# Compression weights of the second mixer: read unsplit as fp32 moving operands, with the block rows in four 32-column groups of the array

## The reference, cut to what matters

```python
def nsa_compress(k, pos, w1, w2):
    n_cmp = (seq - CMP_LEN) // CMP_STRIDE + 1            # 15
    idx = np.arange(n_cmp)[:, None] * CMP_STRIDE + np.arange(CMP_LEN)[None, :]
    blk = jnp.swapaxes(k[:, idx], 2, 3) + pos.astype(k.dtype)
    flat = blk.reshape(bsz, n_cmp, g, CMP_LEN * dk)      # 2 groups x 15 windows = 30 rows of 2048
    return jax.nn.gelu(flat @ w1, approximate=True) @ w2  # w1: 2048 x 256
```

## Time and profile before

| what | value |
| --- | --- |
| time, median of 3 runs | 2051.24 us (2049.7 to 2053.11) |
| span of the profiled execution | 2053.3 us, 2.1 us over that median |
| TensorE busy | 2039.6 us, 99% of the span |
| VectorE, ScalarE busy | 1475.2 us (72%), 1152.8 us (56%) |
| granted TensorE clock, mean | 0.998 |

### The profile page before, as it was taken

The page is one execution under the profiler, slowest core; times in us unless marked ns, Lnnn a source line. Parts: engine busy times, 40 slices in busy tenths (PEclk is TensorE's granted clock), DMA queues, the critical chain, the costliest instruction groups (busy, mean ns, idle before and its releaser), DMA issues.

```text
span 2053.3 us, 39877 instructions
## 1 busy us (share of the span) xinstructions
PE 2039.6 (99%) x17337; PEld 1975.7 (96%) x17340; DVE 1475.2 (72%) x1877; ACT 1152.8 (56%) x1459; POOL 129.9 (6%) x114
## 2 busy tenths in 40 slices
PE   9999999999999999999999999999999999999998
PEld 8999899999999999999999999999999999999998
DVE  6556866655655587676557999678778899868776
ACT  5435365534544456564446776756557685756555
POOL 1001000100101010010000000001000000000100
PEclk9999999999999999999999999999999999999999
DMA  7665544666566565366665554455655564445652
GB/s 256 206 206 175 183 144 141 196 198 195 175 207 200 190 193 165 103 200 221 223 200 168 163 165 140 159 175 186 223 191 156 162 199 160 149 151 171 222 186 103
DMA packets 287106, 369.78 MB, mean 180 GB/s; under 512 B 10531, under 2 KB 258771, under 8 KB 286931
## 3 DMA queue, kind: packets, MB, share of 16 engines
q1 hardware_dynamic: 281858, 361.47, 54.1%
q10 hardware_dynamic: 5072, 5.75, 0.9%
HBM read 365.36 MB, written 1.05 MB: 178 GB/s over the span
## 4 chain that ended last, share of the span: by engine, by line
PE 96%; DVE 1%; ACT 1%; DMA 1%; ACTq 0%; issue 0%; DVEq 0%
PE ps L717 28%; PE ps L718 27%; PE ps L719 27%; PE ps L828 1%; PE ps L889 1%; PE ps L887 1%; PE ps L885 1%; PE ps L1259 1%; PE ps L830 1%; PE ps L829 1%; DMA arena<-arena 1%; PE ps L1271 1%; PE ps L1292 1%; ACT whi L1482 1%; PE ps L1079 1%; PE ps L1106 0%
## 5 line engine op out<-in xcount | busy, mean ns | idle before, releaser
L717 PE MATMUL ps<-hhi,whi 128*128 128x256 f32 x3774 | 1056.2, 280 | 1.4 <-DVE hlo L2221 1.3
L718 PE MATMUL ps<-hlo,whi 128*128 128x256 f32 x3774 | 1044.1, 277 | 0.0
L719 PE MATMUL ps<-hhi,wlo 128*128 128x256 f32 x3774 | 1044.0, 277 | 0.0
L2128 DVE TENSOR_TENSOR wlo<-raw,whi 128x2048 fp32r<-128x2048 f32 x341 | 771.9, 2264 | 376.6 <-ACT whi L1482 376.5
L1482 ACT ACTIVATE whi<-raw 128x2048 fp32r<-128x2048 f32 (+2 forms) x346 | 651.4, 1886 | 537.1 <-PE ps L719 441.9
L717 PEld LDWEIGHTS ps<-hhi,whi 128*128 128x128 f32 x3774 | 707.6, 187 | 9.0 <-issue 5.4
L718 PEld LDWEIGHTS ps<-hlo,whi 128*128 128x128 f32 x3774 | 707.7, 188 | 1.2 <-issue 0.5
L719 PEld LDWEIGHTS ps<-hhi,wlo 128*128 128x128 f32 x3774 | 708.0, 188 | 0.2
L717 PE MATMUL ps<-hidhi,whi 128*128 128x256 f32 x880 | 243.3, 276 | 0.0
L719 PE MATMUL ps<-hidhi,wlo 128*128 128x256 f32 x880 | 243.1, 276 | 0.0
L718 PE MATMUL ps<-hidlo,whi 128*128 128x256 f32 x880 | 243.1, 276 | 0.0
(11 more groups left out here) (321 smaller groups left out, 2189.6 us busy)
## 6 DMA issues: line engine op xcount, KB each, us to landing
raw<-in_ffn_w_up SPq DMA_DIRECT2D x88, 1024.0 KB, 5.2
raw<-in_w_in SPq DMA_DIRECT2D x68, 1024.0 KB, 5.2
raw<-in_ffn_w_down SPq DMA_DIRECT2D x66, 1024.0 KB, 5.0
raw<-in_ffn_w_gate SPq DMA_DIRECT2D x43, 1024.0 KB, 5.3
raw<-in_w_gate SPq DMA_DIRECT2D x32, 1024.0 KB, 5.4
raw<-in_w_branch SPq DMA_DIRECT2D x16, 1024.0 KB, 5.0
raw<-in_nsa_cmp_w SPq DMA_DIRECT2D x8, 1024.0 KB, 5.4
raw<-in_w_out SPq DMA_DIRECT2D x6, 1024.0 KB, 5.0
```

Of the source, the lines that this page charges most:

```text
L717: pe.matmul(o, w_hi, m_hi, start=start, stop=False, skip_group_check=True)
L718: pe.matmul(o, w_hi, m_lo, start=False, stop=False, skip_group_check=True)
L719: return pe.matmul(o, w_lo, m_hi, start=False, stop=stop, skip_group_check=True)
L2128: dve.tensor_tensor(wlo[:, slot, 0:n], raw[:, slot, 0:n], whi[:, slot, 0:n].bitcast(F32), ALU.subtract) \
```

## The change

For units 15 to 18 the split is gone: TensorE reads the weights from `raw`, in plain fp32, as the moving operand, and the block rows from `blkf` unsplit, in plain fp32, as the stationary one. One matmul takes the place of three. The eight slices of a unit go in turn to four groups of 32 output partitions of the PSUM bank, so each of four groups of columns of the array holds the rows of its own slices. The four partial sums then stand below one another (126 partitions): ACT copies them out, and the matmul that turned the 30 rows now also adds the four groups, since its moving operand is four identity matrices stacked (`quads`, a new constant). The gelu moves behind the turn.

SP's loads into the slots that these units held wait for `used` (TensorE is done) and no longer for `lo_ready`. The semaphore counts for the later splits are shifted (`splits2`). `pool_avg` moves to another part of its buffer, so that it does not lie over `blkf`.

```diff
+PLAIN_UNITS = tuple(range(M2_W1, M2_GATE))
+QUAD = 32
...
+    quads = (r[:, None] % QUAD) == np.arange(QUAD)[None, :]
...
-        pool_avg = view(pool_flat[:, 3072:4096], g=4, t=SEQ)
+        pool_avg = view(pool_flat[:, 0:1024], g=4, t=SEQ)
...
+            def load2(l, s, n, src):
+
+                slot = s % RING
+                if s - RING in PLAIN_UNITS:
+                    sp.wait_ge(used[slot], uses2(l, s))
+                    sp.dma_start(raw[:, slot, 0:n].rearrange("p (k c) -> p k c", k=src.shape[1]), src) \
+                        .then_inc(raw_ready[slot], 16)
+                else:
+                    load(slot, n, splits2(l, s), src)
...
                     if i == M2_W1:
-                        pe.wait_ge(blk_split, (l + 1) * 2)
-                    slot = i % RING
-                    unit_ready(slot, u(i))
-                    o = bank(4, v * CMP_HID, CMP_HID)[0:KVH * NCMP, :]
+                        pe.wait_ge(blk_ready, (l + 1) * BLK_STEPS)
+                    slot, rows = i % RING, KVH * NCMP
+                    pe.wait_ge(raw_ready[slot], 16 * (uses2(l, i) + 1))
                     for jl in range(CJ // 2):
-                        j = part * (CJ // 2) + jl
-                        w = slice(jl * CMP_HID, (jl + 1) * CMP_HID)
-                        b = slice(j * KVH * NCMP, (j + 1) * KVH * NCMP)
-                        last = mm3(o, blk_hi[:, v, b], blk_lo[:, v, b], whi[:, slot, w], wlo[:, slot, w], j == 0, j == CJ - 1)
+                        j, q = part * (CJ // 2) + jl, jl % 4
+                        n = QUAD if q < 3 else rows
+                        b = (v * CJ + j) * rows
+                        last = pe.matmul(bank(4, v * CMP_HID, CMP_HID)[q * QUAD:q * QUAD + n, :], blk_flat[:, b:b + n],
+                                         raw[:, slot, jl * CMP_HID:(jl + 1) * CMP_HID], start=j < 4, stop=j >= CJ - 4,
+                                         skip_group_check=True)
                     last.then_inc(used[slot], 1)
...
-                    pe.wait_ge(gelu_done, l * 3 + 1)
+                    pe.wait_ge(hid_kept, l + 1)
                     n = KVH * NCMP
                     for x in range(4):
-                        last = pe.matmul(bank(4, x * 32, n), hid_tok[0:n, x * P:(x + 1) * P], ident[0:n, 0:n], start=True, stop=True)
+                        last = pe.matmul(bank(4, x * QUAD, n), hid_tok[0:HID_ROWS, x * P:(x + 1) * P], quads[0:HID_ROWS, 0:n],
+                                         start=True, stop=True)
...
                 def next_split(i):
+                    if i + 2 in PLAIN_UNITS:
+                        return
...
-                        act.activation(hid_tok[0:KVH * NCMP, :], bank(4)[0:KVH * NCMP, :], ACT.Gelu_apprx_tanh).then_inc(gelu_done, 1)
+                        act.activation(hid_tok[0:HID_ROWS, :], bank(4)[0:HID_ROWS, :], ACT.Copy).then_inc(hid_kept, 1)
...
-                    if i == BLK_AT:
-                        for v in range(2):
-                            act.wait_ge(blk_ready, l * BLK_STEPS + (v + 1) * BLK_STEPS // 2)
-                            act.activation(blk_hi[:, v, :], blkf[:, v, :, :, :].rearrange("p j g n -> p (j g n)"), ACT.Copy) \
-                                .then_inc(blk_hi_done, 1)
...
-                                       .rearrange("p x (g n) -> p x g n", g=KVH), ACT.Copy).then_inc(gelu_done, 1)
-                        act.wait_ge(gelu_done, l * 3 + 2)
+                                       .rearrange("p x (g n) -> p x g n", g=KVH), ACT.Gelu_apprx_tanh).then_inc(gelu_done, 1)
+                        act.wait_ge(gelu_done, l * 2 + 1)
```

More of the change, by code:

```diff
@@ L88 @@
 POOL_AT = 15
-BLK_AT = 9
 CONV_FROM = 7
@@ L164 @@
                       ("causal", 3 * P), ("window", 3 * P), ("cmpadd", TT * CP), ("cmp01", TT * CP),
-                      ("blockdiag", P), ("half", 2)])
+                      ("blockdiag", P), ("half", 2), ("quads", QUAD)])
 POOL_COLS = SEQ + P
@@ L387, in hybrid_network @@
         on_half = table(C2_AT, "half", 2)
+        quads = table(C2_AT, "quads", QUAD)
         def par_rows(i, r, n, src):
@@ L526, in uses2, with splits2, unsplit @@
             return DEPTH * (L1_UNITS // RING) + l * (L2_UNITS // RING) + s // RING
+        def splits2(l, s):
+            def unsplit(before):
+                return sum(x % RING == s % RING for x in PLAIN_UNITS if x < before)
+            return uses2(l, s) - l * unsplit(L2_UNITS) - unsplit(s)
         def bank1_of(i):
@@ L626, in conv_load @@
                 def conv_load(s, src):
-                    load(s % RING, UNIT, uses2(l, M2_END + s), src)
+                    load2(l, M2_END + s, UNIT, src)
                 def gate(p):
@@ L686, in _ @@
                         src = A["nsa_cmp_w1_2"][bass.ds(l, 1), v, part * D:(part + 1) * D, :]
-                        load(s % RING, UNIT, uses2(l, s), src.rearrange("a (j p) c -> p (a j) c", p=P))
+                        load2(l, s, UNIT, src.rearrange("a (j p) c -> p (a j) c", p=P))
                         s += 1
@@ L695, in _ @@
                                 .rearrange("k p c -> p k c")
-                        load(s % RING, UNIT, uses2(l, s), src)
+                        load2(l, s, UNIT, src)
                         s += 1
@@ L700, in _ @@
                         src = w[bass.ds(l * (NBR * BRC * P) + (n * BRC * P + i * UC), UC), :]
-                        load(s % RING, UNIT, uses2(l, s), src.rearrange("(k p) c -> p k c", p=P))
+                        load2(l, s, UNIT, src.rearrange("(k p) c -> p k c", p=P))
                         s += 1
-                out_proj(l, uses2, s, A["w_o_2"])
+                out_proj(l, splits2, s, A["w_o_2"])
                 conv_ffn(l)
@@ L2728, in turn @@
                                                       ALU.add).then_inc(blk_ready, 1)
-                def blk_low():
-                    for v in range(2):
-                        dve.wait_ge(blk_hi_done, l * 2 + v + 1)
-                        dve.tensor_tensor(blk_lo[:, v, :], blkf[:, v, :, :, :].rearrange("p j g n -> p (j g n)"),
-                                          blk_hi[:, v, :].bitcast(F32), ALU.subtract).then_inc(blk_split, 1)
                 def softmax(j):
```

45 lines of the change are left out of this document (23 added, 22 removed).

## The result

The changed kernel takes 2055.11 us (median of 9 runs, 2051.55 to 2057.86), beside 2051.18 us of the kernel before (9 runs). The ratio is 1.0017 with a 95% interval of 1.0009 to 1.0025: **slower by 3.9 us**, 1.8 to 5.1. It is inside the forecast's range, 4.7 us above its point, and on the slower side of no change, by a small amount that the interval does tell from zero.

A forecast was written before the change was run, and what follows sets the result against it. TensorE, busy 99% of the span, bounds the kernel. Of 13.3 us saved in matmuls, late loads leave 0.4 us a layer, 0.8 us for two: 2050.4 us, own range 2048.5 to 2054.0, over the cases 2046.0 to 2056.5.

The forecast's parts named there:

- What the matmuls give: Units 15 to 18 on TensorE: four groups at once, 1.1 us a unit, 1.66 us saved, 13.3 us over eight.
- rival (c): Units 15 to 18: one column group at a time, 3.7 us a unit, +13.8 us, 2065.0 us; chance 0.06.
- What the moved loads cost: Unit 19's load 1.0 us later, 4 us wait at `times_v(0)`, unit 20 0.8 us early, 0.4 us a layer kept.
- that half: Half of unit 20's 0.8 us lead taken as kept, 0.4 us a layer, since VectorE is 98% busy until 1240.
- The removed splits: Eight high parts on ScalarE, eight low parts on VectorE and the block rows' split: by themselves worth nothing.
- The clock: Behind the `times_v(0)` wait the clock may fall to half: one fall +0.6 us, two +2.1 us; verdict unmoved.
- both fall: The clock falls behind the `times_v(0)` wait in both layers: +2.1 us, 2053.3 us.
- (a): The gain arrives because the waits do not come; all of it gives 2037.9 us; chance 0.13.
- (b): Units 15 to 18: only two groups at once, 2.0 us a unit, +3.7 us, 2054.9 us; chance 0.12.
- (d): The clock falls in both layers at its full price, 3.4 us each, 2056.4 us; chance 0.06.
- The base: The profiled span of 2053.3 us stood 2.1 us over the runs' median; the forecast step was taken from 2051.24.

The follow-up runs named there:

- Experiment 4: The changed kernel with all eight matmuls of a unit in one column group instead of four; 2068.23 us, ratio 1.0087.
- experiment 1: The changed kernel with filler matmuls, 16 ahead of `times_v(0)` and 2 ahead of `hidden_turn`; 2051.24 us, ratio 0.9999.
- experiment 7: The changed kernel with the 16 filler matmuls ahead of `times_v(0)` alone, none at `hidden_turn`; 2049.61 us, ratio 0.9993.
- experiment 8: The changed kernel with unit 19's weights loaded into the free buffer `mixed`, ahead of unit 18's load; 2043.81 us, ratio 0.9962.
- experiment 2: The changed kernel with ScalarE's split of unit 19 moved behind the tanh that `times_v(0)` waits for; 2052.32 us, ratio 1.0005.
- experiment 5: The changed kernel with unit 16's weights in the free buffer `mixed`, unit 19's load issued right behind unit 18's; 2053.35 us, ratio 1.0007.
- experiment 6: The changed kernel with the early loads of experiment 5 and the ScalarE order of experiment 2 together; 2051.15 us, ratio 0.9996.
- experiment 9: The kernel of experiment 8 with ScalarE's split of unit 19 also moved behind its tanh; 2048.78 us, ratio 0.9988.
- experiment 10: The kernel before, weights split and three passes kept, with only the early load of unit 19 from experiment 8; 2051.59 us, ratio 1.0001.
- experiment 3: The changed kernel with `pool_windows` put behind unit 16 instead of ahead of it; 2050.32 us, ratio 0.9993.

## Why the prediction was wrong, step by step

**What the matmuls give: right.** 1.1 us a unit predicted, 1.00 measured. Four groups at once was an assumption beyond the rows, which showed two; it came true. Experiment 4 gives the price without the groups, 3.6 us a unit, and 6.8 to 7.0 us a layer where rival (c) had 6.9.

**What the moved loads cost: right, to 0.1 us in layer 0, as long as the clock holds.** Counted from unit 15, the load of unit 19 goes out at 5.80 us (predicted 5.9), its split starts at 11.23 (11.3), `times_v(0)` at 15.18 (15.1), behind a wait of 4.07 (4). From there on the kernel with fillers shows the same program with the clock holding: unit 19 at 18.60 us (predicted 18.6, from 1186.35), unit 20 at 27.46 (27.46, from 1195.2; 27.80 in layer 1), and VectorE's low part of unit 22 at 34.53 (34.46, from 1202.2). The lead at unit 22 is 0.5 and 0.4 us, where I had taken 0.4 a layer; that half was a choice between 0 and 0.8, so its fit is partly luck. Experiments 1 and 7 are 0.9 and 1.1 us below the kernel before, where I had 0.8.

**The removed splits are worth nothing: not contradicted, not isolated.** No run removes them alone. Part of the 3.7 us a layer of experiment 8 may be theirs; that stays open.

**The clock: this step failed.** I wrote that a wait of 4 us "may do the same, twice", and took the clock as holding for the point. It fell: seen in the profiled execution, and told by the mean clock, 0.995 to 0.997, in all nine runs. The size for one fall was fair: 1.85 us at unit 20 predicted, 1.93 measured in layer 0 (29.39 against 27.46 us with fillers), 1.37 in layer 1 (29.17 against 27.80). What was missing is the second fall of layer 0: the late load of unit 21 turned the predicted 0.5 us at `hidden_turn` into 1.37, half clock came again at 1194.0, and at unit 22 the loss is 2.9 us. So the changed kernel loses 2.9 + 1.3 = 4.2 us to the clock in the profiled execution, and 4.8 or 5.0 us by the medians of experiments 1 and 7, each taken from the kernel before beside it. The case "both fall", written down as +2.1 us and 2053.3, was the real one, and was 1 us too cheap for want of that second fall.

What should have moved the choice was in the rows: the one stall of 3.57 us in the trace had been followed by half clock, so the only evidence said "falls", and nothing in the trace showed a stall of that size without it. I left the two open because both stay within 0.2%; by the rows the point had to be 2053.3 us, 1.8 us from the result, and the chance of slower had to be larger.

**The rivals.** (a) did not come because ScalarE is held at unit 19 as counted; experiment 8 shows that the gain is there once it isn't, and more than half of it arrives (7.5 of 13.3 us). (b) and (c) are out: four groups run at once. (d) put the full price of a fall at 3.4 us a layer, 2056.4; the measured 2.9 and 1.3 lie below it. Its time was closer to the result than my point, since it had the clock falling.

**The base.** I took the span's 2.1 us over the median as the execution's own offset. That held up: the second profile of the kernel before is 4.8 us faster at unit 15, without the stall, and the distances used in the count are equal to 0.03 us.

## What to carry to other kernels

When a change makes TensorE faster in a short stretch, count the loads before anything else: here four units of 8 matmuls went by in less time than their successors' weights needed, and a load that went out 1 us later, where TensorE came almost 5 us sooner, cost the whole gain. Put the transfer that is needed first ahead of the one that has time; two at once are both late (6.5 to 10.3 us for 5.4). And price a new wait of TensorE twice, once for its length and once for the clock behind it: here the 4 us hole of each layer lost 1.3 to 2.9 us on top, and filler matmuls, or the wait cut into pieces under a microsecond, give them back.

## What the runs showed of the hardware that I had not expected

Four column groups fed in turn with plain fp32 run at once: the records of unit 15 start in fours, within 0.02 us of one another and 0.22 to 0.24 us behind the four before, and 16 of them of 256 columns take 1.07 us, against 3.64 us in one group. The way into and out of the groups costs little: 1.00 us from the first record to the next line's first.

The length of a wait alone does not say whether the clock falls. It fell behind the 3.57 us of the earlier trace rows, behind waits of 4.1, 4.2, 4.1, 4.8, 4.8, 4.5, 4.6 and twice 3.16 us (the changed kernel and experiments 2, 5, 6, 9), behind 2.07 us in layer 1 of experiment 10, behind 1.37 us in layer 0 of the changed kernel, and behind the 1.30 us of its start-up, where the twelve other profiles held; it held behind 3.43 us in layer 0 of experiment 5, 2.54 us twice in experiment 3, 1.07 us in layer 0 of experiment 10, 2.0, 2.1, 1.3 and 1.4 in experiment 4, and 0.9 us wherever that stood. But for those in which a kernel ends, the stretches at half clock were 3.4 or 6.8 us long. The Trainium skill ("TensorE: Matmul & The Clock Gate", HAM oscillation — how this bites in real kernels) describes a related pattern: a piece of matmuls that is shorter than the wait for the next transfer, and a lower clock behind each such wait. Here there is one such wait in a layer and not one at each piece. The trace agrees that the price follows the wait, with 13.6 us at half clock behind the changed kernel's waits in the second mixer and none in the same place with experiment 8's loads.
